# Mixer work placed inside the input projections of a four-mixer transformer kernel

## The reference

```python
# even layer: retention (4 heads of 128) beside dilated attention (8 heads of 64)
rq, rk, rv, rg, dq, dk, dv = _split(h @ w_in, EVEN_SIZES)
rq, rk = _rotary(rq), _rotary(rk) * RET_DK ** -0.5
o_r = _head_norm(_retention(rq, rk, rv)) * silu(rg)
dq, dk = _rotary(dq), _rotary(dk)          # 16 of 64 columns turn
o_d = _dilated_attention(dq, dk, dv)       # softmax over three patterns
out = concatenate([o_r, o_d]) @ w_out
# odd layer: gated linear attention (4 heads, keys 128, values 256, chunks of 64)
q, k, v, r, a_low = _split(h @ w_in, GLA_SIZES)
log_a = log_sigmoid(a_low @ w_a2 + b_a) / 16
o = _head_norm(_gla(q, k, v, log_a)) * silu(r)
out = o @ w_out
# head norm: (o - mean) * rsqrt(var + eps), per head and token
```

## Time and profile before

| | us |
|---|---|
| median of 3 runs | 3020.01 (3019.6 to 3020.63) |
| the profiled execution | 3020.34 |
| its span, first to last instruction | 3018.5 |
| mean granted clock of TensorE | 0.954 of 2.4 GHz |
| busy: TensorE, DVE, ACT, POOL | 2836.0, 1788.6, 1227.7, 191.3 |
| even mixer: projection; from there to its output projection | 2020.2 to 2100.9; to 2198.1 |
| gated linear mixer: the same | 2611.8 to 2680.8; to 2787.6 |

### The profile page before, as it was taken

One profiled execution on the slowest core, in us unless ns is written; L12 is line 12 of the kernel. 1 busy time (PEld: TensorE's weight loads), 2 busy tenths in 40 slices (PEclk: granted clock), 3 DMA queues, 4 the chain that ended last, 5 costly groups with the idle time before them and its releaser, 6 DMA issues.

```text
span 3018.5 us, 45651 instructions
## 1 busy us (share of the span) xinstructions
PE 2836.0 (94%) x17144; PEld 2478.8 (82%) x17144; DVE 1788.6 (59%) x2709; ACT 1227.7 (41%) x1822; POOL 191.3 (6%) x239
## 2 busy tenths in 40 slices
PE   5999989989999899998989998999799999976998
PEld 2888876678888788887859998998499999975998
DVE  6977345758772487425376555556456566653664
ACT  3433223732222333223255545543355455432553
POOL 0100010011000010001001010010000000000001
PEclk8999999999999999999999998999589999985999
DMA  6666222026652266333204564565036555530554
GB/s 253 205 194 189 93 78 84 1 79 218 191 178 95 95 214 190 120 96 109 91 28 142 184 183 133 177 202 173 1 121 186 180 183 178 189 111 0 167 178 129
DMA packets 119315, 424.13 MB, mean 141 GB/s; under 512 B 13408, under 2 KB 14448, under 8 KB 119072
## 3 DMA queue, kind: packets, MB, share of 16 engines
q1 hardware_dynamic: 98640, 351.32, 37.2%
q0 software_dynamic: 19520, 70.19, 7.6%
q10 hardware_dynamic: 1040, 1.05, 0.1%
HBM read 421.45 MB, written 1.05 MB: 140 GB/s over the span
## 4 chain that ended last, share of the span: by engine, by line
PE 88%; DVE 7%; ACT 3%; issue 1%; DMA 1%; POOL 0%; DVEq 0%; ACTq 0%; POOLq 0%
PE bank L723 27%; PE bank L724 27%; PE bank L725 27%; DVE rstd L1661 1%; DVE WL L1487 1%; PE bank L869 1%; ACT WH L1174 1%; DVE g_max L1804 1%; PE bank L764 1%; DMA xT<-in_xT 1%; DVE d_small L1866 0%; PE bank L709 0%; DVE tn L1771 0%; PE bank L958 0%; PE bank L888 0%
## 5 line engine op out<-in xcount | busy, mean ns | idle before, releaser
L723 PE MATMUL bank<-XH,WH 128*128 128x256 f32 (+1 forms) x3776 | 1229.6, 326 | 62.3 <-DVE XL L1680 44.3
L724 PE MATMUL bank<-XL,WH 128*128 128x256 f32 (+1 forms) x3776 | 1221.5, 323 | 0.0
L725 PE MATMUL bank<-XH,WL 128*128 128x256 f32 (+1 forms) x3776 | 1220.9, 323 | 0.0
L1487 DVE TENSOR_TENSOR WL<-raw,WH 128x1024 fp32r<-128x1024 f32 (+1 forms) x664 | 803.6, 1211 | 685.5 <-ACT WH L1174 682.1
L1174 ACT ACTIVATE WH<-raw 128x1024 fp32r<-128x1024 f32 (+1 forms) x664 | 683.7, 1035 | 872.4 <-PE bank L725 869.3
L723 PEld LDWEIGHTS bank<-XH,WH 128*128 128x128 f32 x3776 | 728.7, 193 | 124.1 <-issue 53.6
L724 PEld LDWEIGHTS bank<-XL,WH 128*128 128x128 f32 x3776 | 728.9, 193 | 54.6 <-issue 1.9
L725 PEld LDWEIGHTS bank<-XH,WL 128*128 128x128 f32 x3776 | 728.4, 193 | 53.2
L725 PE MATMUL bank<-HH,WL 128*128 128x256 f32 (+1 forms) x1408 | 459.3, 326 | 0.0
L724 PE MATMUL bank<-HL,WH 128*128 128x256 f32 (+1 forms) x1408 | 457.1, 325 | 0.0
L723 PE MATMUL bank<-HH,WH 128*128 128x256 f32 (+1 forms) x1408 | 453.7, 322 | 0.0
(11 more groups left out here) (301 smaller groups left out, 1674.4 us busy)
## 6 DMA issues: line engine op xcount, KB each, us to landing
a_rows<-in_ada_t POOLq DMA_DIRECT2D x124, 512.0 KB, 4.0
raw<-in_ffn_w_gate SPq DMA_DIRECT2D x88, 512.0 KB, 3.6
raw<-in_ffn_w_up SPq DMA_DIRECT2D x88, 512.0 KB, 4.3
raw<-in_ffn_w_down SPq DMA_DIRECT2D x64, 512.0 KB, 3.5
raw<-in_ffn_pre_w_gate SPq DMA_DIRECT2D x44, 512.0 KB, 3.5
raw<-in_ffn_pre_w_up SPq DMA_DIRECT2D x44, 512.0 KB, 3.9
raw<-in_ffn_post_w_gate SPq DMA_DIRECT2D x44, 512.0 KB, 3.5
raw<-in_ffn_post_w_up SPq DMA_DIRECT2D x44, 512.0 KB, 4.2
```

Of the source, the lines that this page charges most:

```text
L723: nc.tensor.matmul(o, WH[:, j % 4, k, :], high, start=start, stop=False)
L724: nc.tensor.matmul(o, WH[:, j % 4, k, :], low, start=False, stop=False)
L725: return nc.tensor.matmul(o, WL[:, j % 4, k, :], high, start=False, stop=stop)
L1487: nc.vector.tensor_tensor(WL[:, b, 0:d, :], raw[:, b, 0:d, :], WH[:, b, 0:d, :].bitcast(F32), ALU.subtract).then_inc(split_done, 1)
```

## The change

The projections of `mix2` and `mix3` are written out tile by tile and get side work. The order of the even projection becomes dilated queries, keys, values, then retention's queries and keys, values, gates. Each rotary covers two tiles in one product into bank 7, with its cosine on POOL. The 19 steps of dilated attention use banks 4, 5, 6 once each and bank 7 for pairs; 17 of them stand behind tiles 11 to 27. V turns into banks 6 and 7. For the gated linear mixer, the low-rank product, the gates, sums, V and key turns and decays stand behind tiles 2 to 22. The mean of a head's output is taken out by centring the values (`ret_centre`, `gla_vc`) instead of the outputs. After the projection only the heads remain: products, outputs, squares from the bank, gate, variance, root, reciprocal, scale, high and low half, in one software pipeline of stages over the heads on each engine; the sigmoid gates are written in place, and the tables for Silu and Sqrt are loaded once each. The gated linear heads use bank halves so that two heads' states are in flight.

The core of the diff:

```diff
+        GLA_SIDE = {(0, 2): [("wsplit", 0)], (1, 0): [("low", 0)], (1, 1): [("lowc", 0)], (1, 2): [("z", 0)],
+                    (1, 3): [("z", 1), ("znabs", 0)], (2, 0): [("znabs", 1)], (2, 1): [("softplus", 0)], (2, 3): [("la", 0)],
+                    (3, 0): [("sums", 0)], (3, 1): [("v", 0), ("b", 0)], (3, 2): [("v", 1), ("eb", 0), ("bd", 0)],
+                    (3, 3): [("en", 0), ("qt", 0)], (4, 0): [("v", 2), ("ko", 0)], (4, 1): [("v", 3), ("kt", 0)],
+                    (4, 2): [("kturn", 0), ("vc", 0)], (4, 3): [("vc", 1)], (5, 0): [("silu", 0), ("vc", 2)],
+                    (5, 1): [("silu", 1), ("vc", 3)], (5, 2): [("silu", 2)]}
+        RET_SIDE = {}
+        for at_slot, item in ((4, ("rope", 0)), (5, ("rope", 1)), (8, ("rope", 2)), (9, ("rope", 3)), (12, ("v", 0)), (12, ("v", 1)),
+                              (16, ("rope", 4)), (18, ("rope", 5)), (20, ("rope", 6)), (22, ("rope", 7)), (24, ("v", 2)),
+                              (25, ("centre", 0)), (26, ("v", 3)), (27, ("centre", 1)), (27, ("silu", 0))):
+            RET_SIDE.setdefault((at_slot // 4, at_slot % 4), []).append(item)
+        for n in range(17):
+            RET_SIDE.setdefault(((11 + n) // 4, (11 + n) % 4), []).append(("dil", n))
...
-                mixer(2, n, [("ab_w_in_2", 7, S, r_proj, 0)], "ab_w_out_2", S, gate2(1))
+                mixer(2, n, [("ab_w_in_2", 7, S, r_proj, 0, [4, 5, 6, 0, 1, 2, 3], RET_SIDE)], "ab_w_out_2", S, gate2(1))
             else:
-                mixer(3, n, [("gla_w_in_2", 6, S, a_proj, 0)], "gla_w_out_2", S, gate2(1))
+                mixer(3, n, [("gla_w_in_2", 6, S, a_proj, 0, None, GLA_SIDE)], "gla_w_out_2", S, gate2(1))
...
+        def first_v(m, n):
+            return (24, 8)[n // 2] if m == 2 else 8 + 4 * (n // 2)
+        def rope_bank(m, n):
+            return bank[7] if m == 2 else bank[4 + n % 2]
...
+        def v_bank(m, n):
+            return bank[6 if n == 1 else 7] if m == 2 else bank[6 + n % 2]
...
+                    if m == 2:
+                        free_seven()
+                        seven["v"] += 1
+                    if m >= 2:
+                        for d in range(4):
+                            pe.wait_ge(*evicted(g, first_v(m, n) + d))
...
+            seven = {"rope": 0, "v": 0, "pair": 0}
+            def free_seven():
+                if seven["rope"]:
+                    pe.wait_ge(rot_read[2], seven["rope"])
+                if seven["v"]:
+                    pe.wait_ge(v_stored[2], seven["v"])
+                if seven["pair"]:
+                    pe.wait_ge(dil_out, seven["pair"])
...
+            def dil_step(n):
+                if n < len(L_JOBS):
+                    h, t = L_JOBS[n]
+                    r0 = 64 * (h % 2)
+                    if h % 4 == 0 and t == 0:
+                        pe.wait_ge(roped[2], 3 + h // 4)
+                    if n >= 1:
+                        pe.wait_ge(l_sem["nm"], n)
+                    nc.tensor.matmul(bank[4][:, 0:S], r_proj[r0:r0 + 64, 16 + h // 2, t * P:(t + 1) * P],
+                                     r_proj[r0:r0 + 64, 20 + h // 2, :], start=True, stop=True).then_inc(l_sem["scores"], 1)
+                if 1 <= n <= len(L_JOBS):
+                    s = n - 1
+                    pe.wait_ge(l_sem["exp"], s + 1)
+                    if s >= 1:
+                        pe.wait_ge(l_sem["pt"], s)
+                    for c in range(2):
+                        last = nc.tensor.transpose(bank[5][:, c * P:(c + 1) * P], l_s[:, s % 4, c * P:(c + 1) * P], ident[:, :])
+                    last.then_inc(l_sem["turned"], 1)
+                if 2 <= n < len(L_JOBS) + 2:
+                    s = n - 2
+                    h, t = L_JOBS[s]
+                    pe.wait_ge(l_sem["pt"], s + 1)
+                    if s == 0:
+                        pe.wait_ge(v_stored[2], 2)
                     else:
...
+                        pe.wait_ge(l_sem["o_read"], s)
+                    for c in range(2):
+                        last = nc.tensor.matmul(bank[6][:, 0:64], l_pt[:, s % 2, c * P:(c + 1) * P],
+                                                r_vn[:, c, 512 + h * 64:512 + h * 64 + 64], start=(c == 0), stop=(c == 1))
+                    last.then_inc(l_sem["o_done"], 1)
+                o = dil_pair(n - 3)
+                if o is not None:
+                    pe.wait_ge(l_sem["o_read"], n - 2)
+                    free_seven()
+                    seven["pair"] += 1
+                    for t in range(2):
+                        last = nc.tensor.transpose(bank[7][:, t * P:(t + 1) * P], l_o[:, t, o * P:(o + 1) * P], ident[:, :])
+                    last.then_inc(l_sem["o_turned"], 1)
...
+            def ret_out(h):
+                pe.wait_ge(ret_masked, h + 1)
+                if h >= 2:
+                    pe.wait_ge(rs["og"], h - 1)
+                o = bank[2 + h % 2]
+                nc.tensor.matmul(o[:, 0:256], r_vn[:, 0, h * P:(h + 1) * P], r_sm[:, h % 2, 0:256], start=True, stop=False)
+                nc.tensor.matmul(o[:, P:256], r_vn[:, 1, h * P:(h + 1) * P], r_sm[:, h % 2, 256:384], start=False,
+                                 stop=True).then_inc(ret_o, 1)
...
             def mix2():
-                pe.wait_ge(tables, tables_at[2])
                 banks_free(last_proj[2])
...
                 pe.wait_ge(roped[2], len(ropes[2]))
...
+                ret_products(0)
+                dil_step(17)
+                ret_products(1)
+                pe.wait_ge(rs["vc"], 2)
+                for s in range(1, H_RET + 2):
+                    if s <= H_RET:
+                        ret_out(s - 1)
+                    if s == 1:
+                        dil_step(18)
+                        pe.wait_ge(l_sem["o_read"], len(L_JOBS))
+                    if s + 1 < H_RET:
+                        ret_products(s + 1)
+                    if s >= 2:
+                        ret_var(s - 2)
...
+            def gla_var(h):
+                pe.wait_ge(gs["sq"], h + 1)
+                if h >= 2:
+                    pe.wait_ge(gs["root"], h - 1)
+                for e in range(2):
+                    last = nc.tensor.matmul(bank[6 + h % 2][:, 0:S], ones_e[:, :], sq[:, h % 2, e * S:(e + 1) * S], start=(e == 0),
+                                            stop=(e == 1))
+                last.then_inc(gs["var"], 1)
+            def mix3():
+                banks_free(last_proj[3])
+                pe.wait_ge(gs["qt"], 1)
+                pe.wait_ge(gs["kt"], 1)
                 pe.wait_ge(gs["kstore"], 2)
...
+                for s in range(H_GLA + 2):
+                    if s < H_GLA:
+                        gla_state_products(s)
+                    if 1 <= s <= H_GLA:
+                        gla_out(s - 1)
+                    if s >= 2:
+                        gla_var(s - 2)
...
+                elif what == "softplus":
+                    act.wait_ge(gs["znabs"], 2)
+                    link(nc.scalar.activation(a_la[:, :, :], a_la[:, :, :], ACTF.Exp))
+                    nc.scalar.activation(a_la[:, :, :], a_la[:, :, :], ACTF.Ln, bias=ones_1[:, 0:1]).then_inc(gs["ln"], 1)
...
+            def dil_step(n):
+                if 1 <= n <= len(L_JOBS):
+                    s = n - 1
+                    act.wait_ge(l_sem["turned"], s + 1)
+                    if s >= 2:
+                        act.wait_ge(l_sem["o_done"], s - 1)
+                    nc.scalar.activation(l_pt[:, s % 2, :], bank[5][:, 0:S], ACTF.Copy).then_inc(l_sem["pt"], 1)
+                if n < len(L_JOBS):
+                    act.wait_ge(l_sem["nm"], n + 1)
+                    nc.scalar.activation(l_s[:, n % 4, :], l_s[:, n % 4, :], ACTF.Exp, bias=l_small[:, n, 0:1], scale=HD ** -0.5,
+                                         accum_out=l_small[:, n, 2:3]).then_inc(l_sem["exp"], 1)
...
+            def dil_step(n):
+                if n < len(L_JOBS):
+                    sm = l_small[:, n, :]
+                    if n >= 4:
+                        dve.wait_ge(l_sem["turned"], n - 3)
+                    dve.wait_ge(l_sem["scores"], n + 1)
+                    link(nc.vector.tensor_tensor_reduce(out=l_s[:, n % 4, :], in0=bank[4][:, 0:S], in1=r_dmask[:, L_JOBS[n][1], :], scale=1.0,
+                                                        scalar=-3e38, op0=ALU.add, op1=ALU.max, accum_out=sm[:, 6:7]))
+                    nc.vector.tensor_scalar(sm[:, 0:1], sm[:, 6:7], -HD ** -0.5, None, ALU.mult).then_inc(l_sem["nm"], 1)
+                if 1 <= n <= len(L_JOBS):
+                    sm = l_small[:, n - 1, :]
+                    dve.wait_ge(l_sem["exp"], n)
+                    nc.vector.reciprocal(sm[:, 6:7], sm[:, 2:3]).then_inc(l_sem["rec"], 1)
+                if 2 <= n < len(L_JOBS) + 2:
+                    s = n - 2
+                    h, t = L_JOBS[s]
+                    dve.wait_ge(l_sem["o_done"], s + 1)
+                    dve.wait_ge(l_sem["rec"], s + 1)
```

(47 more changed lines are left out.)

647 lines of the change are left out of this document (244 added, 403 removed).

## The result

| | before, us | after, us |
|---|---|---|
| median of the runs beside each other | 3019.81 (3019.51 to 3020.63) | 2915.19 (2915.06 to 2916.67) |
| ratio | | 0.9654 (95%: 0.9638 to 0.9671) |
| the profiled execution, its span | 3020.34, 3018.5 | 2915.17, 2913.4 |

The profiled execution is 105.2 us shorter; 91.7 were forecast.

A forecast was written before the change was run, and what follows sets the result against it. TensorE was taken to bound the kernel, with two mixer stretches (204 us) mostly at 1.2 GHz. Gains of 38.8 (even) and 52.9 us (gated linear), 91.7 together, gave 2929 us, range 2908 to 2964.

The forecast's parts named there:

- Part 1: Even mixer, work moved into the projection: 29.6 us of side work (bounds 27 to 33) plus 4.7 of stalls.
- The tables: Even projection: the last table lands at 2034.4, the first rotary stands at 2034.6; no wait, a microsecond at risk.
- Part 2: Even mixer's tail after the last tile: 26 us (bounds 22 to 31), less 1.9 back in the output projection.
- Part 3: Gated linear mixer, work moved into the projection: 10.9 us of TensorE plus 5 of stalls (bounds 1 to 12).
- The rule that was weighed and left out: Every ACT table switch adds a drain of about 1.38 us; the estimate would be 2935 instead of 2929.
- Part 4: Gated linear mixer's tail: 38 us taken (bounds 30 and 46), from 44 at the low clock and 31 at the high.
- Rival 3: Both tails stay at 2.4 GHz (38 to 31, 26 to 23), side work cheap, stalls 3 less: 2916 us; chance 0.2.
- Rival 2: DVE and ACT chain closes too late: attention slots stall 1.5 us each, gated linear slots 10 in all; 2960; chance 0.15.
- Rival 1: Clock falls to 1.2 GHz in both projections from the first side item on, costing 138 us: 3066; chance 0.03.
- The signs: Even, gated linear projections 112 to 118, 83 to 88 us; tails 22 to 28, 34 to 42; even clock 1.00.

The follow-up runs named there:

- the filled run above: Kernel after, with 17 dilated attention steps put behind the even projection and ten unread products filling TensorE's idle after the first step: 2915.3 us (0.9656).
- the run with the idle: Kernel after, with a DVE delay ahead of the four gated linear heads that leaves TensorE idle: 2929.6 us (0.9708).

## Why the prediction was right, and where it was off

**Part 1, right.** 36.1 us for 34.3. Stalls are 4.4, the forecast's own sum, and that is part luck: the V turns waited 1.30 and 1.55 (1.3 and 2.1 foreseen), one turn or rotary behind a pair 0.6 (twice 0.5 foreseen), and 0.9 at the second rotary was not foreseen. There TensorE waits for DVE to read the first rotary, and DVE's low weights ahead of that took 2.28 us in place of 1.22 while GpSimd multiplied a cosine. Side work is so 31.7, in the bounds of 27 to 33: a plain step costs 1.43 (4.31 less 2.88), not 1.26. Half the duration at 1.2 GHz leaves out starts and waits that do not shrink. The tables cost no wait.

**Part 2, off by 3.8.** DVE's first mask is done 4.8 us after the last tile (5.3 foreseen). Then masks and gates run ahead of the roots, and at the end a head costs DVE a reciprocal, a scale, a low half and perhaps a gate, 2.8 us (2150.66 to 2153.45), and 2.45 without the gate, not 3.9: the forecast counted every step of a head in each round, though masks and some gates fall into time when DVE waits anyway.

```profile
2150.66 1.74 DVE L1928 RECIPROCAL tn<-tn 128x256 f32<-128x256 f32 x1
2152.44 0.42 DVE L1929 TENSOR_TENSOR r_o<-r_o,tn 128x256 f32<-128x256 f32 x1
2152.78 0.42 DVE L1933 TENSOR_TENSOR XL<-r_o,XH 128x256 fp32r<-128x256 f32 x1
2153.12 0.42 DVE L1919 TENSOR_TENSOR r_o<-bank,r_proj 128x256 f32<-128x256 f32 x1
2153.45 1.74 DVE L1928 RECIPROCAL tn<-tn 128x256 f32<-128x256 f32 x1
```

**Part 3, right.** 14.8 for 15.9. The sums waited 2.2 us (3.3), the split 0.8 (0.8). The rule that was weighed and left out, the drain of The Trainium skill, page ScalarE: Activation LUTs, section What ACT_TABLE_LOAD costs, does not show: the load starts 0.02 us after the cast ends, and the exponential behind it 1.29 later.

```profile
2607.70 1.06 ACT L1196 ACTIVATE WH<-raw 128x1024 fp32r<-128x1024 f32 x1 [1.82 <-PE bank L709]
2608.78 1.28 ACT L1240 ACT_TABLE_LOAD   x1
2610.07 1.06 ACT L1240 ACTIVATE a_la<-a_la 128x1024 f32<-128x1024 f32 x1
```

**Part 4, the step that failed.** The text had both numbers, 31 at the high and 44 at the low clock, and took 38 (bounds 30 and 46; measured 27.9) because "the same products held 0.50 for 34.4 us before". That row was read as a property of the products. The runs show that the stage's past decides: in them a stream of these heads stayed for long at the level at which it found the clock (19.4 and 21 us at 0.50 with TensorE full; all of it at 1.00 when entered at 1.00), and one wait of 2.04 us between the products lost it. The kernel before had both, the idle of 6.03 us ahead and waits of 0.9 in every head; which of them held it down there is not shown. The change enters the tail at 1.00 and its pipeline leaves no wait over 0.6 us until the last variance. Even the 31 was too long (its own terms, 2.5 + 25 + 4.7, make 32): TensorE (4.85 a head), not DVE (6.3), paces until 2675, since DVE works off its reciprocals behind.

**Rivals.** Rival 3 came true for the gated linear tail alone; the even one was short for another reason, with a clock of 0.78, and side work was not cheap (31.7 for 29.6). That the time fell on its 2916 is part luck. Rival 2 did not come: 0.91 us of slack held. Rival 1 was drawn from the low clock of small products standing alone, and the filled run above has those at 1.00; it exists in the gated linear projection of some executions, at 3.4 us, and not in the even one.

**The signs.** Both projections (116.8 and 83.8 us at 1.00) came as foretold, and none of their idles reached 3 us. Both tails left their windows on the short side: 21.6 us for 22 to 28, and 27.7 for 34 to 42.

What exactly brings the clock back stays open. In four places it rose during or within 2 us of products over 128 rows and 256 columns (variances, retention), but no run changed only that, and there are cases against it: with the heads one after another the states behind the third variance still took 2.07 us, and split products of that shape in the output projection of the run with the idle stood at 1.2 GHz for some 6 us (2697.16 to 2703.1) before it rose.

## What to carry to other kernels

Where a stretch runs at 1.2 GHz, look at the idle ahead of it before taking the level for a property of its work: keep TensorE fed at the seam (a few products that nobody reads were worth 18 us in one place) or leave no wait in the stage. Moving work into a stage where TensorE is full pays by the chain's waits and by the clock, not by hiding TensorE's time; each moved attention step still cost 1.43 us. Filling is no cure by itself: behind the norms a fall cost 1.5 to 2.8 us, and a filling where there is no idle costs its full length.

## What the runs showed of the hardware

- One idle of 3.29 us was followed by 40 us at 1.2 GHz with TensorE busy 40.54 of 44.70 us, that idle counted in; ten products in its place kept the same stream at 2.4 GHz. The Trainium skill, page TensorE: Matmul & The Clock Gate, Part 1, ties the level to how busy TensorE has been; in this pair the same stream, with TensorE busy nearly throughout, stood at either level, by what lay ahead of it.
- DVE's low weights take 1.22 us, but 1.87 where GpSimd multiplies a cosine, and 2.28 at the first of these. Timelines of POOL, DVE and PE, after:

```profile
2078.37 1.28 POOL L648 TENSOR_TENSOR sg<-r_proj,r_cos 128x512 f32<-128x512 f32 x1 [7.34 <-DVE r_proj L1620]
```

```profile
2078.87 1.87 DVE L1518 TENSOR_TENSOR WL<-raw,WH 128x1024 fp32r<-128x1024 f32 x1 [0.72 <-ACT WH L1196]
```

```profile
2036.05 2.28 DVE L1518 TENSOR_TENSOR WL<-raw,WH 128x1024 fp32r<-128x1024 f32 x1 [0.86 <-ACT WH L1196]
...
2039.08 1.10 PE L833 MATMUL bank<-r_proj,l_rot 128*128 128x512 f32 x2 [0.86 <-DVE tn L1779]
```

The Trainium skill, page GPSIMD Engine Reference, section 1. Specifications, says that the two share their way to SBUF and contend when DVE reads two inputs there; the rows agree. The forecast gave these products no price. The 0.65 us fell within the slack of the attention slots; at the first of them TensorE waited 0.9 us.
